# Hybrid diffusion trunk on one core: modulation kept on chip as columns, and the prologue's transfers on one queue in the order of their need

## The reference, cut to what matters

```python
mod = (jax.nn.silu(cond) @ lp['ada_w'] + lp['ada_b'])[:, None, :]
sh1, sc1, g1, sh2, sc2, g2 = jnp.split(mod, 6, axis=-1)
xm = rmsnorm(h, lp['norm1']) * (1.0 + sc1) + sh1
proj = xm @ lp['w_in']
...
h = h + g1 * (merged @ lp['w_out'])
xm2 = rmsnorm(h, lp['norm2']) * (1.0 + sc2) + sh2
h = h + g2 * hier_moe(xm2, ...)
```

## Time and profile before

| | |
|---|---|
| median of 3 runs | 2444.15 us (2444.05 to 2445.18) |
| profiled execution, its own time | 2443.61 us |
| its span in the profile | 2441.5 us |
| mean granted TensorE clock | 0.965 of full speed |
| TensorE matmuls busy | 2234.5 us, 92% |
| VectorE, ScalarE, GpSimd busy | 882.0, 554.7, 567.1 us |
| DMA | 368.80 MB, mean 151 GB/s |

### The profile page before, as it was taken

The page is one execution under the profiler, slowest core; times in us unless marked ns, Lnnn a source line. Parts: engine busy times, 40 slices in busy tenths (PEclk is TensorE's granted clock), DMA queues, the critical chain, the costliest instruction groups (busy, mean ns, idle before and its releaser), DMA issues. The chain is left out here.

```text
span 2441.5 us, 32401 instructions
## 1 busy us (share of the span) xinstructions
PE 2234.5 (92%) x12844; PEld 1360.5 (56%) x12844; DVE 882.0 (36%) x1721; ACT 554.7 (23%) x1094; POOL 567.1 (23%) x588
## 2 busy tenths in 40 slices
PE   2999999999999998899959999999999989969992
PEld 1555667776677654333335556777767766533330
DVE  1100456545454335111150007555644433331114
ACT  1100131212444421111130002211134443111112
POOL 0000101325000530555210002033330026045541
PEclk7999999999999999899979999999999999979996
DMA  9333122112110944988763312112221148169855
GB/s 328 147 140 116 37 79 66 51 41 84 51 52 20 361 136 185 383 327 341 243 236 136 121 63 87 57 57 67 61 73 37 34 183 282 50 255 373 317 183 181
DMA packets 189974, 368.80 MB, mean 151 GB/s; under 512 B 54545, under 2 KB 129905, under 8 KB 176129
## 3 DMA queue, kind: packets, MB, share of 16 engines
q1 hardware_dynamic: 135600, 203.04, 24.2%
q0 software_dynamic: 39168, 136.39, 14.7%
q10 hardware_dynamic: 15056, 27.31, 3.3%
HBM read 432.04 MB, written 54.13 MB: 199 GB/s over the span
## 5 line engine op out<-in xcount | busy, mean ns | idle before, releaser
L568 PE MATMUL psum<-arena,h 128*128 128x320 f32 x2048 | 615.0, 442 | 9.5 <-ACT h L586 6.6
L568 PEld LDWEIGHTS psum<-arena,h 128*128 128x128 f32 x2048 | 367.9, 190 | 146.0 <-ACT h L586 10.5
L408 PE MATMUL psum<-arena 128*128 128x413 f32 (+3 forms) x1184 | 388.7, 489 | 0.0
L408 PEld LDWEIGHTS psum<-arena 128*128 128x128 f32 x1184 | 209.9, 192 | 170.9 <-issue 170.9
L1903 PE MATMUL psum<-arena 128*64 128x512 f32 x1152 | 263.5, 611 | 10.6 <-DMA arena<-in_moe_w,wrow 8.2
L1641 POOL DMA_INDIRECT arena<-in_moe_w,wrow x144 | 143.1, 994 | 230.5 <-DVE wrow L2132 187.2
L1903 PEld LDWEIGHTS psum<-arena 128*64 128x64 f32 x1152 | 83.2, 140 | 166.0 <-issue 162.8
L1798 PE MATMUL psum<-arena 128*128 128x320 f32 x512 | 138.8, 433 | 6.2 <-DMA arena<-in_w_branch 3.5
L1809 PE MATMUL psum<-arena 128*128 128x512 f32 x320 | 140.5, 594 | 0.0
L459 DVE COPY arena<-psum 128x413 f32<-128x413 f32 (+2 forms) x36 | 17.6, 490 | 335.9 <-PE psum L408 335.0
L1926 PE MATMUL psum<-arena 128*64 128x512 f32 x576 | 131.4, 598 | 0.9 <-ACT arena L1998 0.9
(11 more groups left out here) (317 smaller groups left out, 2733.2 us busy)
## 6 DMA issues: line engine op xcount, KB each, us to landing
arena<-in_ada_w SPq DMA_DIRECT2D x24, 2048.0 KB, 12.0
h<-in_w_in SPq DMA_DIRECT2D x32, 1024.0 KB, 5.4
gate_rows<-h SPq DMA_DIRECT2D x128, 160.0 KB, 1.8
arena<-gate_rows SPq DMA_DIRECT2D x16, 1280.0 KB, 11.1
y_rows<-arena ACTq DMA_DIRECT2D x72, 256.0 KB, 6.5
arena<-in_w_in SPq DMA_DIRECT2D x8, 1652.0 KB, 7.7
arena<-mod_rows SPq DMA_DIRECT2D x24, 512.0 KB, 7.0
arena<-in_w_branch SPq DMA_DIRECT2D x16, 512.0 KB, 10.1
```

Of the source, the lines that this page charges most:

```text
L408: ins = nc.tensor.matmul(psum[:, 4 + i % 4, 0:w], lhs, rhs, start=(k == 0), stop=(k == KD - 1))
L568: ins = nc.tensor.matmul(psum[:, gate_bank(i), 0:HT], gw[c % 2][:, k, f:f + P], gate_xt[:, k, half:half + HT], start=(k == 0), stop=(k == ...
```

## The change

Shift and scale are no longer brought to all partitions through DRAM. TensorE transposes the rows (`turn_rows`), DVE copies what is needed into 32 small columns `mcol` (`copy_cols`), and they are applied after the transposition of the tokens, where a feature is a partition: ACT's copy from PSUM becomes eight ACTIVATE instructions of 128x128 with `scale` and `bias` columns. DVE's part for each tile shrinks to the reciprocal and one multiplication by a column. In the prologue the tokens move from ACT's queue to SP's; the rows and the context tokens come ahead of the halves of `ada_w`, the latent tokens behind chunk 0; of the constants only the identity is loaded at the start, the rest once the fourth half of `ada_w` has landed. Tile 0 is normed and transposed ahead of the last half. Between the layers ACT computes one square root of a dummy ahead of its first scaled copy.

```diff
+        def turn_rows(rows, b):
+            for i in range(2):
+                for half in range(2):
+                    ins = nc.tensor.transpose(psum[:, b, (2 * i + half) * P:(2 * i + half + 1) * P],
+                                              rows[:, i, half * P:(half + 1) * P], ident)
+            return ins
+        def copy_cols(own, b, done):
+            for i in range(2):
+                src = psum[:, b, 2 * i * P:2 * (i + 1) * P].rearrange("p (w c s) -> p s c w", w=2, c=4)[:, 0:2]
+                own.send(nc.vector.tensor_copy(mcol[:, 2 * i:2 * i + 2, :].rearrange("p s (c w) -> p s c w", c=4), src), done)
...
         def copy_turned(act, own, S, t):
+            st = 0 if t == 0 else 1
             act.wait_ge(S["nt_ps"], t + 1)
-            own.tell(nc.scalar.activation(xt[:, :, t * P:(t + 1) * P],
-                                          bank(2 * (t % 2), 2).rearrange("p (k t) -> p k t", k=KD), ACT.Copy),
-                     S["nt_done"])
+            for k in range(KD):
+                ins = nc.scalar.activation(xt[:, k, t * P:(t + 1) * P], bank(2 * (t % 2), 2)[:, k * P:(k + 1) * P],
+                                           ACT.Identity, bias=mcol[:, st, k:k + 1], scale=mcol[:, 2 + st, k:k + 1])
+                own.send(ins, S["own_a"] if k < KD - 1 else S["nt_done"])
...
-        def modulate(v, own, S, t):
+        def scale_tile(v, own, S, t):
             v.wait_ge(S["std"], t + 1)
             own.link(nc.vector.reciprocal(rstd[:, t:t + 1], rstd[:, t:t + 1]))
-            own.link(nc.vector.scalar_tensor_tensor(xm2[:, t % 2, :], h[:, t, :], rstd[:, t:t + 1], modb[:, st, :],
-                                                    ALU.mult, ALU.mult))
-            own.tell(nc.vector.tensor_tensor(xm2[:, t % 2, :], xm2[:, t % 2, :], modb[:, 2 + st, :], ALU.add), S["xm"])
+            own.tell(nc.vector.tensor_scalar(xm2[:, t % 2, :], h[:, t, :], rstd[:, t:t + 1], None, ALU.mult), S["xm"])
...
+                sp.dma_start(h[:, 0, :], a["x_prompt"][0]).then_inc(PN["ctx_in"], 16)
+                load_ada_rows(sp, 0, 0, 2, biasP, "norm1", gainP, PN["rows0_in"])
                 for n in range(4):
                     load_ada_half(sp, 0, n // 2, n % 2, slotP[n], awP[n])
-                load_ada_rows(sp, 0, 0, 2, biasP, "norm1", gainP, PN["rows0_in"])
                 load_chunk(sp, PN, 0, 0)
-                sp.wait_ge(PN["row0_done"], 2)
-                store_ada(sp, 0, 0, 2, rowsP, PN["stored0"])
-                sp.wait_ge(PN["stored0"], 16 * 2)
-                load_modb(sp, PN, 0)
+                sp.dma_start(h[:, 1:NT, :], a["x_sample"][0].rearrange("(t p) d -> p t d", p=P)).then_inc(PN["lat_in"], 16)
...
+                pe.wait_ge(PN["row0_done"], 2)
+                turn_rows(rowsP, 6).then_inc(PN["cols_ps"], 1)
+                project_all(pe, PN, 1)
...
-                act.dma_start(h[:, 0, :], a["x_prompt"][0]).then_inc(PN["ctx_in"], 16)
-                act.dma_start(h[:, 1:NT, :], a["x_sample"][0].rearrange("(t p) d -> p t d", p=P)).then_inc(PN["lat_in"], 16)
-                act.dma_start(consts[:, :], a["consts"]).then_inc(PN["consts_in"], 16)
+                act.dma_start(consts[:, 0:P], a["consts"][:, 0:P]).then_inc(PN["ident_in"], 16)
...
+                tile_std(own, PN, 0, junkP)
+                act.wait_ge(awP[3], 16)
+                act.dma_start(consts[:, P:], a["consts"][:, P:]).then_inc(PN["consts_in"], 16)
+                act.wait_ge(PN["cols"], 2)
+                copy_turned(act, own, PN, 0)
                 act.wait_ge(PN["lat_in"], 16)
...
                 if l + 1 < DEPTH:
                     modulation(5)
+                    pe.wait_ge(M["row_done"], 3)
+                    turn_rows(rowsM[:, 1:3, :], 3).then_inc(M["cols_ps"], 1)
...
+                own.link(nc.scalar.activation(ss[:, 0:1], eps_col, ACT.Sqrt))
                 weigh(0)
```

More of the change, by code:

```diff
@@ L235, in build @@
         eps_col = sm(0, 1)
+        mcol = sm(20, 4, KD)
         eps64_col = sm(1, 1)
@@ L382, in evacuate, with turn_tile, project_all @@
             return copy(ptok[:, x2, x0:x0 + x1], src[:, 0:x1])
[L384 to L392, removed]
+        def turn_tile(pe, S, t):
+            pe.wait_ge(S["xm"], t + 1)
+            if t >= 2:
+                pe.wait_ge(S["nt_done"], t - 1)
+            for k in range(KD):
+                ins = nc.tensor.transpose(bank(2 * (t % 2), 2)[:, k * P:(k + 1) * P],
+                                          xm2[:, t % 2, k * P:(k + 1) * P], ident)
+            ins.then_inc(S["nt_ps"], 1)
+        def project_all(pe, S, turned):
             def project(i):
@@ L409, in project @@
                 ins.then_inc(S["proj_ps"], 1)
-            turn(0)
+            for t in range(turned, 1):
+                turn_tile(pe, S, t)
             for i in range(len(items)):
-                if i + 1 < NT:
-                    turn(i + 1)
+                if turned <= i + 1 < NT:
+                    turn_tile(pe, S, i + 1)
                 if i < NT:
@@ L505, in _ @@
                 act.wait_ge(PN["ctx_in"], 16)
+                tile_std(own, PN, 0, junkP)
[3 more added lines that the diff above has]
+                copy_turned(act, own, PN, 0)
                 act.wait_ge(PN["lat_in"], 16)
-                for t in range(NT):
+                for t in range(1, NT):
                     tile_std(own, PN, t, junkP)
-                for t in range(NT):
-                    copy_turned(act, own, PN, t)
+                    if t >= 2:
+                        copy_turned(act, own, PN, t - 1)
+                copy_turned(act, own, PN, NT - 1)
                 copy_even(act, own, PN)
@@ L523, in _ @@
                 own.tell(nc.vector.tensor_tensor(cond[:, :, 0:2], cin, sg, ALU.mult), PN["cond_ready"])
+                scale_tile(v, own, PN, 0)
                 v.wait_ge(PN["rows0_in"], 16 * 8)
@@ L526, in _ @@
                     v.wait_ge(PN["mod0_ps"], 2 * i + 2)
-                    ada_row(own, PN["row0_done"], rowsP[:, i, :], i, biasP[:, i, :], gainP if i == 1 else None)
-                v.wait_ge(PN["modb"], 64)
-                for t in range(NT):
-                    modulate(v, own, PN, t)
+                    ada_row(own, PN["row0_done"], rowsP[:, i, :], 4 + i, biasP[:, i, :], gainP if i == 1 else None)
+                v.wait_ge(PN["cols_ps"], 1)
+                copy_cols(own, 6, PN["cols"])
+                for t in range(1, NT):
+                    scale_tile(v, own, PN, t)
                 copy_odd(v, own, PN)
@@ L2165, in merge_vector @@
                     ada_row(own, M["row_done"], rowsM[:, r, :], bank_of_row[r], biasM[:, r, :], gainM if r == 2 else None)
+                if l + 1 < DEPTH:
+                    v.wait_ge(M["cols_ps"], 1)
+                    copy_cols(own, 3, M["cols"])
+                    own.settle(M["cols"])
             def experts_vector(v):
@@ L2213, in experts_vector @@
                         else:
-                            modulate(v, own, X, t - 1)
+                            scale_tile(v, own, X, t - 1)
                 if not last:
```

34 lines of the change are left out of this document (15 added, 19 removed).

## The result

| | before | after |
|---|---|---|
| median (runs) | 2444.66 us (4: 2444.05 to 2447.17) | 2430.43 us (4: 2429.55 to 2434.03) |
| profiled execution's own time | 2443.61 us | 2430.09 us |
| span | 2441.5 us | 2428.0 us |
| mean granted TensorE clock | 0.965 | 0.966 |

The ratio is 0.9943, with a 95% interval from 0.9928 to 0.9959: the changed kernel is faster by 14.2 us, or 0.57%.

The account below looks back on a forecast made before the run. TensorE, busy 92% of the span, bounds the kernel, so only its idle time yields gains: 13.0 us in the prologue plus 3.5 between the layers, 16.5 us, giving 2427.6 us (0.68% less), range 2421 to 2434.

Parts of the forecast that it names:

- When the halves land: Prologue: `ada_w` halves begin to flow at 9.2 us, bytes through at 29.7, fourth half on TensorE at 31.5 us.
- Tile 0 in columns: Prologue: from the fourth half through columns, transposes and eight ACTIVATE, 8.9 us; tile 0 in `xt` at about 40.5 us.
- The latent tokens: Prologue: tokens behind halves and chunk 0, also paying for constants on ACT's queue, land at 44.1 us.
- rival with independent queues: Prologue: constants leave the tokens untouched, which land at 40.4 us; under the rival of earlier tokens, 3.7 us less, chance 0.2.
- Tile 1: Prologue: from tokens landed, 2.6 us for norm, reciprocal and multiplication, then 1.8 to the first item at 48.5 us.
- Behind it: Items after the first: ACT's 4.4 us and VectorE's 1.0 per tile stay hidden behind TensorE's 6.6 us.
- Between the layers: Before layer 1's first item: VectorE's modulation per tile falls from 2.78 to 1.0 us, gaining 3.5 us.
- The dummy at nothing: Between the layers: the dummy square root lies in ACT's wait for the gathers, table load was hidden: gains nothing.
- The columns between merge and experts at nothing: End of layer 0's merge: added row transposes hide in TensorE's 4.70 us wait for gathered tokens; without cover, 2.4 us cost.
- two terms that I named: The prologue's earlier first item, gain 13.0 us, and the shorter modulation between the layers, gain 3.5 us.
- likeliest case: Whole kernel: the forecast itself, 2427.6 us with its own range 2424 to 2431, chance 0.57.
- second rival of the prediction: Prologue: conditioning vectors hold up the one queue's head, halves start 3 us later, 2433 us; chance 0.16.

Follow-up runs that it names:

- second series: Four more kernels on one chip with their own runs of the kernel before (2442.87 us); the changed kernel, run again unaltered there, took 2426.88 us, ratio 0.994.
- consts_late: The changed kernel with the rest of the constants issued only when the latent tokens have landed: 2427.11 us, ratio 0.9933.
- order_only: The kernel before with only the new order of the prologue's transfers, scale and shift still through DRAM: 2442.53 us, ratio 0.9994.
- tokens_first: The changed kernel with latent tokens ahead of chunk 0, tile 1's norm ahead of tile 0's copies, constants behind the last copy: 2423.47 us, ratio 0.9917.
- halves_first: As tokens_first, with the first two halves of `ada_w` also ahead of the context tokens and small rows: 2423.06 us, ratio 0.9917.
- no_dummy: The changed kernel without the square root of a dummy ahead of ScalarE's first scaled copy: 2430.23 us, ratio 0.9952.
- columns_early: As columns_only, but tiles 0 and 1 multiplied ahead of the rows and transposed behind the third half: 2428.06 us, ratio 0.9938.
- columns_only: The changed kernel with the old queues and transfer order, all five tiles turned after the rows: 2431.03 us, ratio 0.995.

## Why the prediction was right

The forecast was 2427.6 us with a range from 2421 to 2434; 2430.43 was measured, and 2426.88 in the second series, where the kernel before was 1.8 us lower too. The mechanism is the one that was forecast; the total is less exact than its parts, and in the first series lies near the upper end of the forecast's own range (2424 to 2431). Step by step:

- **When the halves land.** 31.5 forecast, 30.57 measured. The flow began sooner than I had taken it: each small row took 0.42 us to issue instead of 0.44 and 0.76, and the first half was issued at 6.28 us instead of 7.2.
- **Tile 0 in columns.** 40.5 forecast, 38.95 measured. The half took 3.34 us, the four transposes 0.66 for 1.0, and the two copies together 0.26 for 0.4. The eight copies of ScalarE are right to the digit: 2.90.
- **The latent tokens.** 44.1 forecast, 44.01 measured. This close a hit is partly luck, since two misses cancel in it. The DMA view of the kernel after, 0 to 40 us, in slices of 1 us:

```profile
GB/s 0 1 68 95 324 328 148 98 295 422 422 418 418 422 410 414 414 401 410 414 410 406 406 418 414 401 410 414 380 351 352 354 353 390 410 489 397 390 486 340
```

These slices sum to 13.9 MB. What stands ahead of the tokens' end on both queues is some 14.7 MB (small transfers and context tokens 1.0, halves 8.39, chunk 0 1.69, latent tokens 2.10, constants 1.52). At 400 GB/s it would be through near 42.0 us, an estimate, since later chunks may hold a share of the slices: 1.4 us sooner than the 43.4 of the prediction. The landing then came some 2 us behind the bytes, and not 0.7. That the tokens pay for the constants is shown: the constants landed 9.5 us after their issue, at 40.1, and consts_late confirms the term, 3.6 us for 3.7. The rival with independent queues would have shown 40.4. The Trainium skill has it so too (DMA: Bandwidth & Descriptors, "Issuing engines are not separate DMA queues"); the runs agree with it, and add the price: the whole time of the other queue's bytes.

- **Tile 1.** 4.4 forecast from the tokens to the item, 4.27 measured; the multiplication took 0.75 us for 0.8. First item at 48.5, measured 48.28: a gain of 13.2 for 13.0.
- **Behind it.** No gap between the five items, and one item at the lower clock. ScalarE's greater part stays hidden.
- **Between the layers.** 3.5 forecast, 3.60 measured. The term missed the item behind it, which took 6.38 us instead of 7.74 at a better granted clock (0.89 for 0.73). These 1.36 us are luck: the item takes 6.23 to 7.71 us in the eight executions with columns.
- **The dummy at nothing.** Right at its place: 15.26 us from the first `fuse` to the item without it, 15.27 with it.
- **The columns between merge and experts at nothing.** The transposes of the rows stand at 970.52, with a wait of 1.09 us, and 3.59 us of waiting for the gathered tokens are left behind them, against 4.70 in the earlier trace rows. The cover held.

The sum, 16.5 us, is 3.0 above the 13.5 of the profiled executions. The two terms that I named are right within 0.2 us each; what the sum left out is what comes back along the way: 1.1 us for the cached value, 0.8 at the end of merge, 1.1 in one expert block, 1.5 near 1532 us, less 1.36 at layer 1's first item. That is 3.1 lost, net. None of it is work that the change adds, but some of it comes with the change. That these losses fall at random from execution to execution holds only for a part of them:

- The wait for `in_cache_gqa_v` stands in the trace of each kernel with columns, 0.9 to 1.5 us in eight executions of seven kernels; in order_only it is 0.2, and before 0. The transfer is not issued later, 2.6 us ahead of the place where TensorE would have gone on (557.67 for 560.27), and 2.7 before (570.83 for 573.51). It lands later: 3.5 to 3.9 us after its issue in the kernels with columns, 3.0 in order_only, 2.6 before. What in the columns brings that about was not tried, and is open. How early TensorE comes there does not size it: the wait is 1.2 us with a lead of 13 (after) and 1.2 to 1.4 with one of 20 (tokens_first, halves_first).
- The merge's slower pieces vary: L1842 took 2.81 us in the changed kernel and 1.96 in its second profile. So does the expert block, 9.88 and 8.78.
- The stretch near 1532 took 9.50 to 9.51 us in the two executions of the changed kernel and in no_dummy, and 7.87 to 7.88 in the five other kernels with columns (8.03 before). These five have their lower clock elsewhere: over 1500 to 1560 us all eight executions with columns show 0.94, the kernel before and order_only 0.97. What shifts the clock there stays open.

No other term of the working was off by more than 1.6 us, and the likeliest case was the one that came. The step that was mis-sized is the passage from the two gains to the total: the prediction added them up as if nothing on the way would take any of it back, and 3.0 of 16.5 us went there.

## What to carry to other kernels

When the operands of a scale and shift vary along the free axis, look whether a transposition follows: behind it they are one number per partition, the broadcast through DRAM goes, and nearly the whole gain here (0.50% of 0.57% by the medians, with intervals that overlap) came from that alone. The order on one queue is then worth what the last transfer ahead of the first real item is worth: ask what the first item needs, put exactly that in front (here tokens ahead of the weights' chunk, constants behind both: 3.4 us more by the medians of one series, with intervals that just touch), and remember that a second queue shares the same bytes per second. Do not count an early start in full. In the four kernels whose first item started 3 to 9 us ahead of the changed kernel's, it took 0.7 to 1.4 us longer, and not in proportion to the lead: 1.4 for 3.9 us (columns_early), 0.7 for 7.6 (tokens_first). In tokens_first and consts_late more of the lead went in later stages.

## What the runs showed of the hardware

- **The first item's length goes with the granted clock of its own stretch.** The same 16 matmuls took 5.81 us at 1.00 (columns_only), 6.83 at 0.83 (after), 7.68 at 0.75 (halves_first), 7.85 at 0.72 (consts_late) and 8.22 at 0.70 (columns_early). In columns_only 3.61 us of transposes and a wait of 1.43 stood ahead of it, in columns_early a wait of 3.40. The two ends as windows, of columns_only and of columns_early:

```profile
49.05:54.70 5.65, 5.65 (x16) 3.10 (x17) 0.00 (x0) 2.74 (x8) 0.00 (x0) 1.00 1.16 323
```

```profile
44.38:52.44 8.06, 8.06 (x17) 4.18 (x18) 0.00 (x0) 2.74 (x8) 0.00 (x0) 0.70 1.11 345
```

- **Tiny transfers at the head of a queue came late when the other queue moved large ones.** The conditioning vectors, 4 KB each, were there for ScalarE at 4.0 to 4.7 us in the kernels with the tokens on the same queue behind them, at 9.73 before, and at 15.11 and 15.10 in columns_only and columns_early, with the same two queues as before. ScalarE's row of columns_only:

```profile
15.11 0.22 ACT L513 ACTIVATE arena<-arena 128x16 f32<-128x16 f32 x1 [11.42 <-DMA arena<-in_c]
```

The queue was not held up at its head, which was the second rival of the prediction: the first half came at 14.07 us, where it would have been 3 us later. Why the vectors needed 15 us twice and 9.7 once with the same transfers is open.
- **Eight small ACTIVATE cost nearly three large ones.** Eight of 128x128, with a column for scale and one for bias, take 2.90 us, while one over 128x1024 takes 1.06 (L436): 0.36 for each against 0.13 for an eighth. It pays here only because ScalarE has time left, 4.4 us for each tile against TensorE's 6.6.
